# Interleaving the Strassen products of the MLP two at a time, and moving four subtractions from GpSimd to VectorE

## The reference

```python
xn = rms_norm(x, norm1_w)
aq, ak, av, mq, mk, mv, mo, mi, mf = split_in(xn @ w_in)      # attention heads and mLSTM heads
...                                                          # differential attention, mLSTM recurrence
x = x + concat([att, ml]) @ w_out
hn = rms_norm(x, norm2_w)
x = x + square(relu(hn @ w_up)) @ w_down                      # 2048 -> 8192 -> 2048
```

## Time and profile before

| | |
|---|---|
| three timed runs | 2426.3, 2427.5, 2427.5 us; median 2427.5 |
| the profiled execution | 2426.36 us, its span 2424.8 us |
| mean granted clock of TensorE | 0.998 |
| PE busy | 2400.3 us (99%) |
| DVE busy | 1776.0 us (73%) |
| ACT busy | 1084.8 us (45%) |
| GpSimd busy | 353.1 us (15%) |
| MLP stage | from about 1049 us to the end |

### The profile page before, as it was taken

How to read it: one execution, slowest core, us unless ns; L and a number is a source line. 1 busy time by engine, 2 the same in 40 slices (tenths; PEclk the granted TensorE clock), 3 DMA queues, 4 the chain that set the end, 5 groups by cost and what they waited for, 6 DMA issues and landing times.

```text
span 2424.8 us, 48650 instructions
## 1 busy us (share of the span) xinstructions
PE 2400.3 (99%) x18890; PEld 2373.9 (98%) x18890; DVE 1776.0 (73%) x2568; ACT 1084.8 (45%) x1715; POOL 353.1 (15%) x408
## 2 busy tenths in 40 slices
PE   8999999999999999999999999999899999999999
PEld 8999999999999999989999999999899999999999
DVE  7466566665657664498888888888888888888887
ACT  5345353453534443364444444444544444444443
POOL 0000000000000100142222222222211101011110
PEclk9999999999999999999999999999999999999999
DMA  5423323333332524424434444444855555655554
GB/s 182 121 82 116 101 88 96 99 103 88 101 104 87 166 86 124 137 97 153 147 136 137 146 144 152 152 152 136 280 155 167 162 166 174 180 180 173 170 164 120
DMA packets 116109, 334.69 MB, mean 138 GB/s; under 512 B 13048, under 2 KB 20856, under 8 KB 116000
## 3 DMA queue, kind: packets, MB, share of 16 engines
q1 hardware_dynamic: 88352, 222.14, 28.0%
q0 software_dynamic: 26208, 106.60, 15.4%
q10 hardware_dynamic: 1440, 4.47, 0.5%
HBM read 274.07 MB, written 59.09 MB: 137 GB/s over the span
## 4 chain that ended last, share of the span: by engine, by line
PE 96%; DVE 2%; issue 1%; DMA 1%; ACT 0%; SPq 0%; DVEq 0%; ACTq 0%
PE psum L639 35%; PE psum L875 18%; PE psum L879 18%; PE psum L877 18%; DVE forms_lo L1767 1%; PE psum L795 1%; PE psum L664 1%; PE psum L721 1%; PE psum L735 1%; PE psum L764 1%; PE psum L679 0%; PE psum L697 0%; PE psum L695 0%; DMA form_raw<-hidden_forms 0%; PE psum L713 0%
## 5 line engine op out<-in xcount | busy, mean ns | idle before, releaser
L875 PE MATMUL psum<-forms_hi,wp_hi 128*128 128x272 f32 x3528 | 1024.6, 290 | 13.1 <-issue 8.9
L879 PE MATMUL psum<-forms_hi,wp_lo 128*128 128x272 f32 x3528 | 1022.5, 290 | 0.0
L877 PE MATMUL psum<-forms_lo,wp_hi 128*128 128x272 f32 x3528 | 1017.4, 288 | 0.0
L639 PE MATMUL psum<-act_tiles,w_hi 128*128 128x272 f32 x4544 | 758.5, 289 | 0.0
L875 PEld LDWEIGHTS psum<-forms_hi,wp_hi 128*128 128x128 f32 x3528 | 665.6, 189 | 14.6 <-issue 9.6
L877 PEld LDWEIGHTS psum<-forms_lo,wp_hi 128*128 128x128 f32 x3528 | 666.7, 189 | 0.0
L879 PEld LDWEIGHTS psum<-forms_hi,wp_lo 128*128 128x128 f32 x3528 | 665.4, 189 | 0.0
L639 PEld LDWEIGHTS psum<-act_tiles,w_hi 128*128 128x128 f32 x4544 | 642.7, 188 | 6.9 <-issue 4.0
L1200 ACT ACTIVATE wp_hi<-ws 128x1024 fp32r<-128x1024 f32 x252 | 267.3, 1061 | 625.3 <-DVE ws L1787 289.9
L639 PE MATMUL psum<-act_tiles,w_lo 128*128 128x272 f32 x2272 | 468.7, 288 | 0.0
L1755 DVE TENSOR_TENSOR wp_lo<-ws,wp_hi 128x1024 fp32r<-128x1024 f32 x252 | 309.6, 1229 | 89.0 <-ACT wp_hi L1200 87.7
(11 more groups left out here) (319 smaller groups left out, 2105.8 us busy)
## 6 DMA issues: line engine op xcount, KB each, us to landing
wa<-in_wpairs SPq DMA_DIRECT2D x248, 512.0 KB, 4.4
w_raw<-in_wstream SPq DMA_DIRECT2D x291, 256.0 KB, 2.7
hidden_forms<-hid POOLq DMA_DIRECT2D x32, 952.0 KB, 4.2
hid<-hidden_forms POOLq DMA_DIRECT2D x31, 952.0 KB, 6.8
out_yT<-cbuf POOLq DMA_DIRECT2D x62, 272.0 KB, 4.6
form_raw<-hidden_forms SPq DMA_DIRECT2D x7, 1088.0 KB, 10.1
res<-in_xT POOLq DMA_DIRECT2D x16, 272.0 KB, 3.9
kc_sb<-in_kcT POOLq DMA_DIRECT2D x8, 512.0 KB, 4.3
```

Of the source, the lines that this page charges most:

```text
L639: last = nc.tensor.matmul(out[0:m, half, :], w[:, w_slot, col:col + m], x[:, half * HB:(half + 1) * HB], start=start and n_ == 0, stop=sto ...
L875: nc.tensor.matmul(bank, wp_hi[:, w, s], form_hi(i)[:, k, :], start=i < 3 and k == 0, stop=False, skip_group_check=True)
L877: nc.tensor.matmul(bank, wp_hi[:, w, s], form_lo(i)[:, k, :], start=False, stop=False, skip_group_check=True)
L879: last = nc.tensor.matmul(bank, wp_lo[:, w, s], form_hi(i)[:, k, :], start=False, stop=k == HALF - 1, skip_group_check=True)
```

## The change

The order and the banks of the seven products change, and who computes the four hidden terms. PE now works on two products at a time: `two_products(p, i)` alternates one matmul of the second half of product `i` (K tiles 4 to 7) with one of the first half of product `i + 1` (K tiles 0 to 3). The waits for product `i + 1` (`begin`) therefore stand 24 matmuls before product `i` has ended. Steps 1 and 32, whose forms come in piece by piece, stay in the old order, with a half product at each seam. Products use four banks in the order y, x, z, 4, y, x, z; product 3 starts a bank of its own, product 5 starts bank x anew. DVE's list in a step is put in another order: low part 6 goes ahead of `c22`, and `sum_1` behind it. The four hidden operations of pair `p - 1` go from GpSimd to DVE, ahead of `c22` of pair `p`; those of the last pair come behind `c22` of the first down step and ahead of its first refill. GpSimd keeps the wait and the store.

```diff
                 def hidden_forms(p):                      # GpSimd
                     pool.wait_ge(squared, (p * 4 + 4).v)
-                    nc.gpsimd.tensor_tensor(h[:, 2, :], h[:, 0, :], h[:, 7, :], ALU.subtract).then_inc(term_ready, 1)
-                    nc.gpsimd.tensor_tensor(h[:, 3, :], h[:, 7, :], h[:, 6, :], ALU.subtract).then_inc(term_ready, 1)
-                    pool.wait_ge(term_ready, (p * 4 + 1).v)
-                    nc.gpsimd.tensor_tensor(h[:, 1, :], h[:, 6, :], h[:, 2, :], ALU.add).then_inc(term_ready, 1)
-                    pool.wait_ge(term_ready, (p * 4 + 3).v)
-                    nc.gpsimd.tensor_tensor(h[:, 5, :], h[:, 4, :], h[:, 1, :], ALU.subtract).then_inc(term_ready, 1)
                     pool.wait_ge(term_ready, (p * 4 + 4).v)
                     pool.dma_start(hid_dram[...], h[:, 0:7, :]).then_inc(hid_stored[b], 16)
...
+                def begin(p, i):                          # PE
                     pe.wait_ge(wp_lo_ready, (p * 7 + (PLACE[i] - 2)).v)
                     if i < 3:
                         pe.wait_ge((c11_done, c21_done, c12_done)[i], p.v)
                     elif i < 6:
-                        pe.wait_ge((u_done, y_copied, v_done)[i - 3], p.v)
+                        pe.wait_ge((c22_done, y_copied, u_done)[i - 3], p.v)
                     else:
                         pe.wait_ge(c22_done, (p + 1).v)
+                    if p.first >= PAIRS + 1 and i in (0, 3, 5):
+                        pe.wait_ge(refill_lo, ((p + (-PAIRS)) * 3 + {0: -2, 3: -1, 5: 0}[i]).v)
...
+                def two_products(p, i):
+                    after = (p, i + 1) if i < 6 else (p + 1, 0)
+                    begin(*after)
+                    for k in range(HALF // 2):
+                        for n_ in range(3):
+                            last = partial(i, k + HALF // 2, n_)
+                            if k == HALF // 2 - 1 and n_ == 2:
+                                last.then_inc(product_done, 1)
+                            partial(after[1], k, n_)
...
                 for i in range(7):
                     product(Step(1), i, 2 * FORM_AT[i])
+                early, late = range(HALF // 2), range(HALF // 2, HALF)
+                product(Step(2), 0, ks=early)
+                with pe.Fori(0, PAIRS - 3) as r:
+                    for i in range(7):
+                        two_products(Step(2, 1, r), i)
+                for i in range(6):
+                    two_products(Step(PAIRS - 1), i)
+                product(Step(PAIRS - 1), 6, ks=late)
+                for i in range(7):
+                    product(Step(PAIRS), i, 2 * (FORMS_UP + i))
+                product(Step(PAIRS + 1), 0, ks=early)
...                                                        # the down loop likewise
+                def hidden_terms(p):                      # DVE: the four operations taken from GpSimd
+                    h = hid[:, p.mod(2)]
+                    dve.wait_ge(squared, (p * 4 + 4).v)
...
                 def c22(p):
+                    dve.wait_ge(u_done, p.v)
                     dve.wait_ge(product_done, (p * 7 + 4).v)
-                    nc.vector.tensor_tensor(cbuf[:, 1, 1, :], bank_x, y_first[:], ALU.subtract).then_inc(v_done, 1)
+                    nc.vector.tensor_tensor(cbuf[:, 1, 0, :], bank_4, x_first[:], ALU.add).then_inc(v_done, 1)
                     dve.wait_ge(v_done, p.v)
-                    nc.vector.tensor_tensor(cbuf[:, 1, 1, :], cbuf[:, 1, 1, :], bank_z, ALU.subtract).then_inc(c22_done, 1)
+                    nc.vector.tensor_tensor(cbuf[:, 1, 1, :], cbuf[:, 1, 0, :], bank_z, ALU.subtract).then_inc(c22_done, 1)
...                                                        # up(p)
                     sum_4(p)
                     if first:
                         form_lo_part(5, FORM_AT[5])
-                    sum_1(p + 1)
-                    dve.wait_ge(squared, (p * 4).v)
+                    wp_lo_part(p, 6)
+                    hidden_terms(p + (-1))
                     c22(p)
                     relu(p, cbuf[:, 1, 1, :], 1, c22_done)
-                    wp_lo_part(p, 6)
+                    sum_1(p + 1)
...                                                        # down(t)
-                    sum_1(p + 1)
-                    refill(t, 0)
+                    wp_lo_part(p, 6)
                     if first:
                         dve.wait_ge(squared, 4 * PAIRS)
                     else:
                         dve.wait_ge(top_added, (t * 16).v)
                     c22(p)
-                    wp_lo_part(p, 6)
+                    if first:
+                        hidden_terms(Step(PAIRS - 1))
+                    refill(t, 0)
+                    sum_1(p + 1)
```

More of the change, by code:

```diff
@@ L99 @@
 PLACE = (0, 1, 3, 4, 5, 2, 6)
+STARTS = (True, True, True, True, False, True, False)
 FREE_AFTER = (-3, -2, 0, 1, 2, -1, 3)
@@ L203, in build @@
         bank_y, bank_x, bank_z, bank_4 = (psum[:, i, 0:HB] for i in range(4))
+        BANKS = (bank_y, bank_x, bank_z, bank_4, bank_y, bank_x, bank_z)
         b11, b12, b21, b22 = (res[:, k, t] for k in (slice(HALF, KT), slice(0, HALF))
@@ L858, in norm2_sum @@
                     sum_rows(ones, (acc,), 0).then_inc(norm_done, 1)
-                def product(p, i, k_ready=None):
-                    bank = (bank_y, bank_x, bank_z, bank_x, bank_y, bank_x, bank_z)[i]
+                def begin(p, i):
                     pe.wait_ge(wp_lo_ready, (p * 7 + (PLACE[i] - 2)).v)
@@ L866, in product, with partial @@
                     elif i < 6:
-                        pe.wait_ge((u_done, y_copied, v_done)[i - 3], p.v)
+                        pe.wait_ge((c22_done, y_copied, u_done)[i - 3], p.v)
                     else:
                         pe.wait_ge(c22_done, (p + 1).v)
-                    for k in range(HALF):
+                    if p.first >= PAIRS + 1 and i in (0, 3, 5):
+                        pe.wait_ge(refill_lo, ((p + (-PAIRS)) * 3 + {0: -2, 3: -1, 5: 0}[i]).v)
+                def partial(i, k, n_):
+                    s, w = slice(k * P, (k + 1) * P), SLOT[i]
+                    weights, form = ((wp_hi, form_hi(i)), (wp_hi, form_lo(i)), (wp_lo, form_hi(i)))[n_]
+                    return nc.tensor.matmul(BANKS[i], weights[:, w, s], form[:, k, :], start=STARTS[i] and k == 0 and n_ == 0,
+                                            stop=k == HALF - 1 and n_ == 2, skip_group_check=True)
@@ L871, in product @@
+                def product(p, i, k_ready=None, ks=range(HALF)):
+                    if ks[0] == 0:
+                        begin(p, i)
+                    for k in ks:
                         if k_ready is not None and k % 4 == 0:
                             pe.wait_ge(form_lo_ready, k_ready + 1 + k // 4)
-                        s = slice(k * P, (k + 1) * P)
-                        w = SLOT[i]
-                        nc.tensor.matmul(bank, wp_hi[:, w, s], form_hi(i)[:, k, :], start=i < 3 and k == 0, stop=False,
-                                         skip_group_check=True)
@@ L877, in product @@
-                        nc.tensor.matmul(bank, wp_hi[:, w, s], form_lo(i)[:, k, :], start=False, stop=False,
-                                         skip_group_check=True)
-                        last = nc.tensor.matmul(bank, wp_lo[:, w, s], form_hi(i)[:, k, :], start=False,
-                                                stop=k == HALF - 1, skip_group_check=True)
-                    last.then_inc(product_done, 1)
+                        for n_ in range(3):
+                            last = partial(i, k, n_)
@@ new lines, in product @@
+                    if ks[-1] == HALF - 1:
+                        last.then_inc(product_done, 1)
[3 more added lines that the diff above has]
+                    for k in range(HALF // 2):
+                        for n_ in range(3):
+                            last = partial(i, k + HALF // 2, n_)
+                            if k == HALF // 2 - 1 and n_ == 2:
+                                last.then_inc(product_done, 1)
+                            partial(after[1], k, n_)
@@ L914, in _ @@
                     product(Step(1), i, 2 * FORM_AT[i])
+                early, late = range(HALF // 2), range(HALF // 2, HALF)
[9 more added lines that the diff above has]
+                product(Step(PAIRS + 1), 0, ks=early)
                 with pe.Fori(0, PAIRS - 2) as r:
                     for i in range(7):
-                        product(Step(2, 1, r), i)
-                for i in range(7):
-                    product(Step(PAIRS), i, 2 * (FORMS_UP + i))
-                def down_step(t):
-                    for i in range(7):
-                        if i in (0, 3, 5):
-                            pe.wait_ge(refill_lo, (t * 3 + (-2, 0, 0, -1, 0, 0)[i]).v)
-                        product(t + PAIRS, i)
-                with pe.Fori(0, PAIRS - 1) as r:
-                    down_step(Step(1, 1, r))
+                        two_products(Step(PAIRS + 1, 1, r), i)
```

(6 more changed lines are left out.)

17 lines of the change are left out of this document (13 added, 4 removed).

## The result

The changed kernel took 2444.6 us (median of 4 runs, 2444.2 to 2445.0) where the kernel before took 2427.5 in the same session: ratio 1.0071, 95% interval 1.0053 to 1.0088. It is slower by 0.7%; 2445 had been forecast. The profiled execution's span is 2443.2 us for 2424.8.

The account below looks back on a forecast made before the run. PE's own pace was taken to bound 61 of 63 steps. Profiled 2426.4 + 6.5 (up) + 0 (down) + 10 (seam) + 1 (entry) = 2443.9, given as 2445 us for the median of runs; range 2424 to 2460.

Parts of the forecast that it names:

- PE's work: About 10,200 matmuls taking turns between two banks, 125.0 ns each instead of 126.1: 11.2 us less if no product waits.
- The up chain: Up stage, product 1's end through VectorE's list to next step's product 3: 21.8 us for 21.0, period 21.4, +6.5 us.
- the short one: Both stages, product 6's end through split 2, sum_3 and low part 3 to product 3: 6.1 us for 6.0.
- The four operations: Hidden operations moved to VectorE in the up stage: 1.55 us a pair, in place of 0.57 from the stretched sum.
- The down stage: Steps after the seam: period 21.2 us, as before, so 0 over 30 steps; bounds -5.7 to +6.
- The chain from product 4: Down stage, from product 4 through the first block's copy and VectorE's list to PE: 12.2 us for four slots, 12.0.
- The seam: Between up and down stages: load queued behind a later store, step 33 begins 6.2 us later; +10 us in all.
- The bound of +14: Upper bound at the seam, if the clock falls after some 10 us of idle PE.
- The entry: Steps 1 and 2: half product +1.5, another wait, less what GpSimd's end gives back; +1 us, estimated -2 to +3.
- Rivals 2 and 3: Chains fit: with the seam still costing 10, 2427 us (20%); with the seam no longer, 2417 us (12%).
- rival 4: VectorE is the bound outright, hidden operations at 2.6 us and down links a little longer: 2463 us (12%).
- rival 5: Turning between banks gives nothing, by the columns rule; slots stay 3.03 us: 2450 us (6%).

Follow-up runs that it names:

- Experiment 3: Kernel before, with K tiles 0 to 3 taking turns with 4 to 7 within each product, all in one bank: 2416.5 us, ratio 0.9956.
- the run with tiles apart: Kernel before, with K tiles in the order 0, 4, 1, 5, 2, 6, 3, 7, three matmuls per tile in a run, one bank: 2416.2 us.
- Experiment 5: Changed kernel, with the four hidden operations ahead of low part 6 in VectorE's list instead of behind it: 2437.5 us, ratio 1.0042.
- Experiment 1: Changed kernel, with the four hidden operations back on GpSimd and the products' order as changed: 2447.95 us, ratio 1.0088.
- Experiment 4: Changed kernel, with the two products of a slot alternating in runs of three matmuls instead of one by one: 2434.2 us, ratio 1.0030.
- Experiment 2: Changed kernel, with GpSimd issuing the first load of hidden forms ahead of its wait for the last pair's terms and store: 2436.9 us, ratio 1.0040.

## Why the prediction was right, and where it was not

- **PE's work.** The size was right: slots of 3.000 us, 125.0 ns a matmul. The cause was not: this is the step of the prediction that failed. The earlier trace rows differ from a normal product in more than the bank: two products take turns there, so the form changes with every matmul and the next K tile comes only after six. I named the one difference that the change is about. Experiment 3 and the run with tiles apart have one bank and 125.0 ns. It did not hurt the time, since the change alters both together, but it hid the better kernel.
- **The up chain.** 21.8 us for 21.0 gave a mean wait of 0.4 and a period of 21.4; measured 0.55 and 0.25 by turns and 21.4, +6.1 us for +6.5. Two small misses cancel in this. Of the 0.55 and 0.25, the second late start has 0.11 each, which the prediction didn't have; the begins themselves were late by 0.44 and 0.14, and worked back from these the chain is 21.0 + 0.44 + 0.14 + 0.11 = 21.7, not 21.8. Experiment 5 took the four operations out of the chain and left the short one.
- **The four operations.** 1.55 us forecast, 1.54 measured; `sum_3` back at 1.22 as forecast. Experiment 1 shows that both together make the move to VectorE a gain in the steps, which the text did not say: it counted them as part of the cost.
- **The down stage.** The term that was mis-sized: 0 forecast, +2.0 measured. The chain from product 4 was right: 12.2 us summed, and in steps 39 to 54 it is 12.18, from the slot's end at 2053.63 to product 3's begin at 2065.81 (two starts of the trace that stand in no row above). But the three slots behind it take 9.11 us and not the 9.0 of the text, because the second matmul behind the wait comes 0.10 late too. That makes 21.29 in 16 steps, +0.10 each, and with 0.3 in step 38 nearly the whole of the 2.0. In the other steps the sum-to-split link is 1.25 instead of the 1.33 of the text, the chain is 12.09, and the period is 21.19. `c22` on VectorE, late by 0.18 where I had taken 0.07 for everything that waits for a product, is not the cause: it is 0.18 in the steps of both kinds. Why the link has two values no run shows. Experiment 4, with 0.25 us more, brings the stage to 21.03.
- **The seam.** +10 forecast, +9.5 measured. Up to step 33's begin it went by the steps given: store at 1766.78, load at 1767.31, ACT 6.8 us later, PE 10.97 us idle, step 33 later by 6.6 us for the 6.2 forecast. The absolute times came 7 us later than the text had them (1778.71 for 1771.3), because it worked in the clock of the kernel before and the up stage had already cost 7. Behind that begin it did not. The text had 1.3 us until product 3 and 3.0 for two half products; product 3 did not wait, and the 2.9 us that came are 0.8 in front of product 1 and the low clock of step 33. That the two come so near each other is luck. Experiment 2 takes the load out from behind the store and gets 7.7 us back. The bound of +14 had allowed for the fall of the clock; it fell (0.83 in that window), but cost no more than it had cost in step 32 of the kernel before.
- **The entry.** +1 forecast, +0.8 measured, but as a difference of larger parts. The text named a half product (+1.5), another wait and something given back; the trace has -3.0 in step 1, +3.5 in step 2 (2.0 us of waiting in front of product 1 and some 15 matmuls at the low clock), +0.6 in step 3. That these come to the +1 is luck.

The sum was 17.5 us over the profiled execution of before, and 18.4 came. Rivals 2 and 3 needed chains that fit, rival 4 hidden operations of 2.6 us, rival 5 a pace of 126.1 ns; each of these is contradicted by a row above.

The rule behind rival 5, from the Trainium skill (TensorE: Matmul & The Clock Gate, section Back-to-back issue gap), knows nothing of banks, and experiment 3 agrees with that so far: 125.0 ns in one bank as in two; its size for the isolated gap, about 116 ns for these columns (an estimate by that rule), no run here shows: they have 125.0 to 126.1.

## What to carry to other kernels

When a change gives a faster pace and an earlier start together, try the pace alone: here the reordering of one loop over K brought 10 us by itself (experiment 3), and with the early start of products, the bank and queue order that went with it, the kernel ended 28 us above that (2444.6 against 2416.5). In a kernel whose bound engine is 99% busy, sum the chains between a resource's release and its next need from start to start, and compare with the time the bound engine gives them; a chain 0.8 us too long in 21 showed as 0.4 us a step. Add to each such wait what comes behind it: here the second matmul, late by another 0.1 us. And look at what stands behind each new wait in a queue: the order of store and load was old, but once the store had to wait for VectorE, the one load behind it cost 7.7 us, as much as some twenty steps of 0.4.

## What the runs showed of the hardware that was not expected

- The pace of a long run of 128x272 matmuls, each with its own weight load, depends on the order of the K tiles: 3.027 us for 24 with tiles 0 to 7, 3.013 with 7 to 0, 3.007 in turns of neighbours, 3.000 with tiles four apart, in turns or in runs of three, in one bank or two. All at the full granted clock.
- A 128x1024 sum on VectorE lasts 1.79 to 1.80 us beside GpSimd's operations on 272 columns and 1.22 without.
- Behind a wait of PE not only the first matmul is late: the second starts 0.22 to 0.23 us after it instead of 0.125, at the full granted clock as well (at product 3 in both stages of the changed kernel).
- A sum on VectorE reaches its ACT split 1.33 us after its start in steps 39 to 54 and 1.25 in the other down steps, in the kernel before, the changed one and that of experiment 4 alike. A done product releases ACT's split 0.08 us after the slot's end in most of the first kind and 0.14 in most of the second; VectorE's `c22` starts 0.18 after it in both.
- A load of 952 KB on GpSimd's queue reached ACT 6.8 us after its issue, in the kernel before and in the changed one, each time directly behind a store of the same size.
